# Gate and up projections of both feed-forward layers in seven block products, tokens in two groups of 528

## What is computed

```python
xp = xp + swiglu(rmsnorm(xp, norm_ffn[l]), w_gate[l], w_up[l], w_down[l])
xs = xs + swiglu(rmsnorm(xs, norm_ffn[l]), w_gate[l], w_up[l], w_down[l])
...
def swiglu(h, wg, wu, wd):
    return (jax.nn.silu(h @ wg) * (h @ wu)) @ wd
```

## Time and profile before

| | us |
|---|---|
| median of 3 runs | 3070.7 |
| the profiled execution | 3068.67 |
| its span, first to last instruction | 3066.9 |
| PE busy in the span | 2811.2 |
| DVE / ACT / POOL busy | 1320.3 / 705.3 / 182.7 |
| PE from first to last matmul of the feed-forward of layer 0 | 924.36 to 1703.15 |

### The profile page before, as it was taken

One profiled execution on the slowest core, in us unless ns is written; L12 is line 12 of the kernel. 1 busy time (PEld: TensorE's weight loads), 2 busy tenths in 40 slices (PEclk: granted clock), 3 DMA queues, 4 the chain that ended last, 5 costly groups with the idle time before them and its releaser, 6 DMA issues. The chain is left out here.

```text
span 3066.9 us, 39415 instructions
## 1 busy us (share of the span) xinstructions
PE 2811.2 (92%) x16574; PEld 2587.3 (84%) x16574; DVE 1320.3 (43%) x1977; ACT 705.3 (23%) x1272; POOL 182.7 (6%) x150
## 2 busy tenths in 40 slices
PE   7999999669799999999999699677889999999998
PEld 5866767647699999999999699654889999999997
DVE  3258997365333332323332534374342332323334
ACT  4133232445312111111111322222221111111110
POOL 1011211000001000000000100060010000000000
PEclk9999999879899999999999799765989999999999
DMA  5312223361511112111110111101111112111111
GB/s 160 96 53 65 90 70 102 131 231 40 200 35 48 42 42 61 44 42 42 42 54 23 37 42 42 33 1 31 56 46 44 42 42 63 42 42 42 42 49 64
DMA packets 222587, 189.49 MB, mean 62 GB/s; under 512 B 24737, under 2 KB 172709, under 8 KB 222399
## 3 DMA queue, kind: packets, MB, share of 16 engines
q1 hardware_dynamic: 220727, 181.80, 19.9%
q0 software_dynamic: 1680, 5.07, 0.5%
HBM read 153.21 MB, written 33.50 MB: 61 GB/s over the span
## 5 line engine op out<-in xcount | busy, mean ns | idle before, releaser
L2684 DVE TENSOR_TENSOR xt<-ps,xt 128x1056 f32<-128x1056 f32 x176 | 221.1, 1256 | 204.1 <-PE ps L2468 204.1
L2468 PE MATMUL ps<-ffn_high,f_whG 128*128 128x352 f32 x1056 | 230.1, 326 | 12.3 <-DVE ffn_low L2398 7.8
L2468 PE MATMUL ps<-f_hidh,f_whD 128*128 128x352 f32 x1056 | 228.6, 325 | 9.9 <-DVE f_wlD L2663 9.9
L2468 PE MATMUL ps<-ffn_low,f_whG 128*128 128x352 f32 x1056 | 229.4, 325 | 0.0
L2468 PE MATMUL ps<-ffn_low,f_whU 128*128 128x352 f32 x1056 | 228.7, 324 | 0.0
L2468 PE MATMUL ps<-f_hidh,f_wlD 128*128 128x352 f32 x1056 | 228.4, 324 | 0.0
L2468 PE MATMUL ps<-f_hidl,f_whD 128*128 128x352 f32 x1056 | 228.2, 324 | 0.0
L2468 PE MATMUL ps<-ffn_high,f_whU 128*128 128x352 f32 x1056 | 227.8, 324 | 0.0
L2468 PE MATMUL ps<-ffn_high,f_wlG 128*128 128x352 f32 x1056 | 227.2, 324 | 0.0
L2468 PE MATMUL ps<-ffn_high,f_wlU 128*128 128x352 f32 x1056 | 226.6, 323 | 0.0
L508 PE MATMUL ps<-pe_wh,even_high 128*128 128x512 f32 (+1 forms) x504 | 206.2, 409 | 3.4 <-POOL pe_wl L367 3.1
(11 more groups left out here) (511 smaller groups left out, 4348.6 us busy)
## 6 DMA issues: line engine op xcount, KB each, us to landing
pe_w<-in_w_in_even_dram SPq DMA_DIRECT2D x56, 256.0 KB, 2.8
proj<-pe_out SPq DMA_DIRECT2D x56, 256.0 KB, 2.0
ht_even<-in_w_gate_dram SPq DMA_DIRECT2D x22, 512.0 KB, 5.1
ht_even<-in_w_up_dram SPq DMA_DIRECT2D x22, 512.0 KB, 6.4
ht_even<-in_w_down_dram SPq DMA_DIRECT2D x22, 512.0 KB
ht_odd<-in_w_gate_dram SPq DMA_DIRECT2D x22, 512.0 KB, 5.2
ht_odd<-in_w_up_dram SPq DMA_DIRECT2D x22, 512.0 KB, 6.5
ht_odd<-in_w_down_dram SPq DMA_DIRECT2D x22, 512.0 KB
```

Source lines behind the costliest of these rows:

```text
L2468: last = pe.matmul(g.ps[0:out_rows, b0 + c, 0:THIRD], lhs, rhs[:, c * THIRD:(c + 1) * THIRD], start=(first and n == 0), stop=(final and n ...
L2684: dve.tensor_tensor(xv, g.ps[:, 3 * (m % 2):3 * (m % 2) + 3, 0:THIRD], xv, ALU.add).then_inc(added, 1)
```

## The change

With A the 256 hidden channels by 1024 inputs of a chunk and B the inputs by 528 tokens, both are cut into 2 by 2 blocks, and the four output blocks come from seven block products in place of eight (the variant with 4 sums on either side). So `stage_ffn` is written anew:
- The tokens go in two groups of 528 (`HALF`), each in two quarters of 264 (`QUARTER`). There are 22 steps n for a layer (11 chunks by 2 groups), and all three weight matrices are loaded, cast and split once per group, twice in all. A load of gate or up is now one of 1 MB for the whole chunk.
- PE: 7 products of gate and 7 of up for each n (`product`, 12 matmuls of 264 columns each), into six PSUM banks in turn; the down projection of step n - 1 in 16 units of 6 matmuls (`down`), in the two other banks, two units behind each of eight of the products. That is 264 matmuls for a step, 5808 for a layer.
- POOL makes 4 weight sums for each matrix and step (`add`, 512 elements a partition) and two of the output sums for each (`cross`, 264 elements).
- ACT casts 14 blocks of 512 elements a step (`cast`) and the down tile twice (`cast_down`), copies 4 products out of PSUM (`copy`), and makes two silus and two casts of 528 (`activate`, `hid`).
- DVE: 14 subtractions of 512 (`low`, called by `lower` for step n + 1), 2 of 1024 (`low_down`), 10 output sums from PSUM (`join`, 264), 2 multiplications and 2 subtractions of 528 (`multiply`, `hid`) and 16 additions to the residual (`add`, 264).
- The token blocks of a group are made once: 8 scalings of 528 (`scale`), 4 differences of 1056 (`difference`), 7 casts and 7 subtractions of 1056 (`token`). `open_first` does it for the first group, `open_second` for the second, at n = 11.
- The first gate chunk is loaded at the end of `stage_project_out`.
- Steps 2 to 8 and 12 to 19 are hardware loops of one step each (7 and 8 turns), the others stand unrolled.

The diff, cut, with the indentation of the added lines shortened (of the removed lines, which are functions of `stage_ffn` before, none is shown):

```diff
+    sp.wait_ge(split, KD)
+    sp.dma_start(g.ht[:, 0:2, :].rearrange("p k n -> p (k n)")[:, 0:2048].rearrange(
+        "p (k n) -> p k n", k=KD),
+                 g.ins["w_gate"][layer][:, 0:2 * P].rearrange("(k p) n -> p k n", p=P)
+                 ).then_inc(g.first_gate, 16)
...
+    JOINED_AT = {"G": {2: 1, 3: 2, 4: 3, 5: 4, 6: 5}, "U": {2: 1, 3: 2, 4: 3, 5: 4, 6: 6}}
+    MULTIPLIED = (5, 7)
+    LOW_ORDER = (0, 1, 3, 4, 2, 5, 6)
...
+def group_chunks(fori, chunk):
+    chunk(0, 0)
+    chunk(1, 0)
+    with fori(0, CHUNKS - 4) as i:
+        chunk(i + 2, 0)
+    chunk(CHUNKS - 2, 0)
+    chunk(CHUNKS - 1, 0)
+    chunk(CHUNKS, 1)
+    with fori(0, CHUNKS - 3) as i:
+        chunk(i + (CHUNKS + 1), 1)
+    chunk(N - 2, 1)
+    chunk(N - 1, 1)
...
+    def chunk(n, group):
...
+            load_down(n - 1, (n - 1) // CHUNKS if isinstance(n, int) else group, 1)
+            if not at(n, N - 2, N - 1):
+                load("G", n + 2, group)
+            load_down(n, group, 0)
+        if not at(n, N - 2, N - 1):
+            load("U", n + 2, group)
...
+    def wait_bank(n, index):
+        if index >= 6:
+            before, index = n, index - 6
+        elif at(n, 0):
+            return
+        else:
+            before, index = n - 1, index + (12 if index < 2 else 6)
+        kind, s = "GU"[index // 7], index % 7
+        if s < 2:
+            pe.wait_ge(copied, 4 * before + COPIES[kind] + s + 1)
+        else:
+            pe.wait_ge(joined[kind], JOINS[kind] * before + JOINED_AT[kind][s])
+    def product(kind, s, n, group):
+        index = FIRST[kind] + s
+        pe.wait_ge(weight_low[kind], 7 * n + LOW_COUNT[s])
+        if at(n, 0, CHUNKS) and kind == "G":
+            pe.wait_ge(token_low, 7 * group + s + 1)
+        if at(n, 0) and index == 5:
+            pe.wait_ge(rep_kept, 1)
+        wait_bank(n, index)
+        out = g.ps[:, index % 6, 0:QUARTER]
+        for j in range(4):
+            a, b = slice(j * P, (j + 1) * P), slice(j * QUARTER, (j + 1) * QUARTER)
+            pe.matmul(out, wh[kind][:, s, a], g.hh[:, s, b], start=(j == 0), stop=False)
+            pe.matmul(out, wh[kind][:, s, a], g.hl[:, s, b], start=False, stop=False)
+            last = pe.matmul(out, wl[kind][:, s, a], g.hh[:, s, b], start=False, stop=(j == 3))
+        last.then_inc(done[kind], 1)
+    def down(n, unit):
+        half, m, t = unit // 8, unit // 2 % 4, unit % 2
+        if unit == 0:
+            pe.wait_ge(hid_low, 2 * n + 2)
+        if unit % 8 == 0:
+            pe.wait_ge(down_low, 2 * n + half + 1)
+        if unit >= 2 or not at(n, 0):
+            pe.wait_ge(added, 16 * n + unit - 1)
+        out, b = g.ps[:, 6 + t, 0:QUARTER], slice(t * QUARTER, (t + 1) * QUARTER)
+        for k in range(2):
+            pe.matmul(out, dh[:, k, m, :], hidh[:, k, b], start=(k == 0), stop=False)
+            pe.matmul(out, dh[:, k, m, :], hidl[:, k, b], start=False, stop=False)
+            last = pe.matmul(out, dl[:, k, m, :], hidh[:, k, b], start=False, stop=(k == 1))
+        last.then_inc(down_made, 1)
+    def chunk(n, group):
+        if at(n, CHUNKS):
+            for u in range(8):
+                down(n - 1, u)
+        u = 8 if at(n, CHUNKS) else 0
+        for kind in "GU":
+            for s in range(7):
+                product(kind, s, n, group)
+                if not at(n, 0) and u < 16 and s in ((3, 4, 5, 6) if kind == "G" else (2, 3, 4, 5)):
+                    down(n - 1, u)
+                    down(n - 1, u + 1)
+                    u += 2
+    group_chunks(pe.Fori, chunk)
+    for u in range(16):
+        down(N - 1, u)
...
+    def add(kind, s, n):
+        pool.wait_ge(raw_in[kind], 16 * n + 16)
+        if not at(n, 0):
+            pool.wait_ge(done[kind], 7 * n - 6 + s)
+        if s in (2, 5):
+            pool.wait_ge(sums[kind], 4 * n + {2: 1, 5: 2}[s])
+        out = four(wsum[kind][:, s, :])
...
+    def cross(kind, n, f):
+        pool.wait_ge(copied, 4 * n + COPIES[kind] + 2)
...
+                pool.wait_ge(hid_low, 2 * n - 1 + f)
+        out = (gate if kind == "G" else prod)[:, f, 1, :]
+        pool.tensor_tensor(out, keep[:, 2 + f, :], keep[:, 1, :], ALU.add).then_inc(crossed, 1)
+    def chunk(n, group):
+        if at(n, 0):
+            for kind in "GU":
+                for s in (1, 2, 4, 5):
+                    add(kind, s, 0)
+        for kind in "GU":
+            if not at(n, N - 1):
+                add(kind, 1, n + 1)
+                add(kind, 2, n + 1)
+            cross(kind, n, 0)
+            cross(kind, n, 1)
+            if not at(n, N - 1):
+                add(kind, 4, n + 1)
+                add(kind, 5, n + 1)
...
+    def cast(kind, s, n):
...
+            src = four(wsum[kind][:, s, :])
+        if not at(n, 0):
+            act.wait_ge(done[kind], 7 * n - 6 + s)
+        act.copy(four(wh[kind][:, s, :]), src).then_inc(weight_high[kind], 1)
...
+            token(1, 4)
+            token(1, 5)
+            token(1, 6)
+        else:
+            cast_down(2 * n - 2, 0, at(n, 1))
+            copy("G", 0, n)
+            copy("G", 1, n)
+        prepare("G", 0, 1, 2, 3, 4)
+        activate(n, 0)
+        prepare("G", 5)
+        activate(n, 1)
+        prepare("G", 6)
+        if not at(n, 0, CHUNKS):
+            cast_down(2 * n - 1, 1)
+        copy("U", 0, n)
+        copy("U", 1, n)
+        prepare("U", 0, 1, 2, 3, 4, 5)
+        hid(n, 0)
+        hid(n, 1)
+        prepare("U", 6)
...
+    def low(kind, s, n):
...
+        src = block_of(kind, *PLAIN[s]) if s in PLAIN else four(wsum[kind][:, s, :])
+        dve.tensor_tensor(four(wl[kind][:, s, :]), src, four(wh[kind][:, s, :].bitcast(F32)), ALU.subtract
+                          ).then_inc(weight_low[kind], 1)
...
+    def hid(n, f):
+        dve.wait_ge(hid_high, 2 * n + f + 1)
+        dve.tensor_tensor(hidl[:, f, :], prod[:, f, :, :].rearrange("p t n -> p (t n)"),
+                          hidh[:, f, :].bitcast(F32), ALU.subtract).then_inc(hid_low, 1)
...
+    def open_first():
...
+                              ALU.mult).then_inc(diagonal, 1)
+        for s in LOW_ORDER[:3]:
+            low("G", s, 0)
+        for k in range(4):
+            scale(0, k)
+        difference(0, 1)
+        token(0, 0)
+        for k in range(4, 8):
+            scale(0, k)
+        dve.tensor_copy(rep[:, :], replicated[:, HALF:T]).then_inc(rep_kept, 1)
+        difference(0, 2)
+        token(0, 1)
+        difference(0, 4)
+        difference(0, 6)
+        token(0, 2)
+        low("G", 4, 0)
+        low("G", 2, 0)
+        token(0, 3)
+        low("G", 5, 0)
+        token(0, 4)
+        low("G", 6, 0)
+        token(0, 5)
+        token(0, 6)
+        for s in LOW_ORDER:
+    def open_second(n):
+        low_down(2 * n - 2)
+        for k in range(4):
+            scale(1, k)
+            add(n - 1, 0, k)
+        difference(1, 1)
+        add(n - 1, 0, 4)
+        token(1, 0)
+        add(n - 1, 0, 5)
+        scale(1, 4)
+        add(n - 1, 0, 6)
+        scale(1, 5)
+        add(n - 1, 0, 7)
+        scale(1, 6)
+        scale(1, 7)
+        difference(1, 2)
+        token(1, 1)
+        difference(1, 4)
+        difference(1, 6)
+        token(1, 2)
+        low_down(2 * n - 1)
+        for s in range(3, 7):
+            token(1, s)
...
+    def chunk(n, group):
...
+        else:
+            low_down(2 * n - 2)
+        lower("G", 0)
+        join("G", 2, n)
+        join("G", 3, n)
+        lower("G", 1)
+        adds(0)
+        lower("G", 3)
+        join("G", 4, n)
+        adds(2)
+        lower("G", 4)
+        join("G", 5, n)
+        adds(4)
+        lower("G", 2)
+        lower("G", 5)
+        join("G", 6, n)
+        adds(6)
+        lower("G", 6)
+        if steady:
+            low_down(2 * n - 1)
+        lower("U", 0)
+        join("U", 2, n)
+        adds(8)
+        lower("U", 1)
+        join("U", 3, n)
+        adds(10)
+        lower("U", 3)
+        join("U", 4, n)
+        adds(12)
+        lower("U", 4)
+        join("U", 5, n)
+        multiply(n, 0)
+        adds(14)
+        lower("U", 2)
+        hid(n, 0)
+        join("U", 6, n)
+        multiply(n, 1)
+        lower("U", 5)
+        hid(n, 1)
+        lower("U", 6)
```

More of the change, by code:

```diff
@@ L2564, in _ @@
+            group_chunks(sp.Fori, chunk)
+            load_down(N - 1, 1, 1)
         @block.tensor
         def _(pe):
-            def hidden(kind, f, first=False):
-                pe.wait_ge(split[kind], f + 1)
-                for k in range(KD):
-                    if first:
-                        wait_normed(pe, k)
-                    last = split_passes(g, pe, 0 if kind == "G" else 3, wh[kind][:, k * P:(k + 1) * P],
-                                        wl[kind][:, k * P:(k + 1) * P], g.hh[:, k, :], g.hl[:, k, :],
-                                        k == 0, k == KD - 1)
-                last.then_inc(made[kind], 1)
@@ L2592, in chunk @@
-            def chunk(c, par):
-                for half in range(2):
```

(57 more changed lines are left out.)

389 lines of the change are left out of this document (230 added, 159 removed).

## The result

The changed kernel takes 3173.65 us, the median of 4 runs (3170.13 to 3176.99), against 3069.57 for the kernel before beside it: a ratio of 1.034 (95% interval 1.0327 to 1.0352). Forecast were 3063 us and a range of 3015 to 3125. The profiled execution has a span of 3169.9 us, 103 more than before.

The account below looks back on a forecast made before the run. PE's columns were taken to bound both feed-forward stages. A layer was 705.1 + 18 + 27 + 17 + 9 = 776 us against 780, 8 us less for both, giving 3063 us, with a range of 3015 to 3125.

Parts of the forecast that it names:

- PE's work: Feed-forward matmuls: 5808 of 264 columns at 121.4 ns, 705.1 us a layer for 767.0, 62 us less.
- The loop turns: 13 hardware-loop turns a layer: between 0 and 0.8 us each, nearest to zero.
- The places of the waits: In each steady step PE was to wait on `low_down` and on the `join` of U6.
- the mechanism: DVE operations with two SBUF operands and POOL's lock each other out, costing between 0 and 1.0 us a meeting.
- the term of the steady step: PE's loss in a steady step: 0.95 us, between 0 and 2.1, in 19 steps, 18 us a layer.
- The walk: Steady step followed operation by operation from U5's end: G1 0.3 us late, `low_down` costing half of 1.2 us.
- start, change of group, end: PE's losses at a layer's start, at step 11 and at its end: 27, 17 and 9 us.
- The clock: Slower rival: a step's wait of 1.2 us drops PE to 1.2 GHz for some 3 us; 3112 us, chance 0.18.
- The slower rival by the chain: DVE reaches U4's `low` late in each step: 2.1 us a step and 0.8 a loop turn; 3127 us, chance 0.12.
- The rival in which the meetings miss: DVE and POOL don't collide harmfully: no loss in a step, starts 5 us shorter; 3017 us, chance 0.24.

Follow-up runs that it names:

- without sums: Changed kernel with POOL's eight weight sums a step left out, their slots filled from a plain block: 3004.8 us.
- both: Changed kernel with DVE's `join` of U5, the first `low_down` and both `hid` moved ahead of `low` operations wanted only next step: 3149.1 us.
- The last kernel: "and step 0" with POOL's up sums waiting for the second `low_down`, and the last down half put into the gate's buffers: 3030.3 us, ratio 0.987.
- and step 0: Variant with DVE's additions early and slack work reordered (3074.7 us), plus step 0's `join` of G6 and ACT's first up copies moved ahead: 3070.5 us.
- the moves of the table: Successive reorderings of DVE's queue, then POOL's up sums delayed and the end shortened, from the changed kernel: 3173.7 us to 3030.3 us.

## Why the prediction failed

**Right:** PE's work. The matmuls of 264 columns lie 120.6 ns apart (36 starts from 1103.65 to 1107.87), forecast 121.4; with no wait a step takes 32.01 us, forecast 32.05. So 62 us a layer were there to be had. The loop turns: taken at nothing, and they cost nothing (32.01 in the loop and in unrolled step 20 without sums; in the changed kernel 35.38 and 35.27). Why is open: no run varies the length of the body, so what the prediction concludes from its number of instructions is not tested. The places of the waits, the `join` of U6 and `low_down`, and the mechanism, two engines that shut each other out.

**Wrong, first: the term of the steady step**, 0.95 us with bounds of 0 and 2.1; it measured 3.37 (35.38 less 32.01), above the upper bound. (The walk's own entries, 0.3 and half of 1.2, make 0.90.) Three entries of the walk were mis-sized:
- `join` of U5 was to start 0.8 us behind U5; it starts at 2.07 (1149.80 less 1147.73). Of the 1.27 us, 0.77 is `low` of U4 meeting POOL's sum of slot 5, 0.26 the sum's own price (1.29 us, not the 1.03 of the earlier trace rows), the rest lags of 0.1 between engines. The walk let this sum collide with `multiply`, behind the `join`, and not with the `low` ahead of it: one operation too late.
- G1 was to be 0.3 late; it is 1.19. That is 0.9 of the 2.4 us by which the term was missed.
- `low_down` was to end at 10.2 if POOL won both times; it ends at 11.77, and the wait is 1.87 us where 1.2 was the full price. That is another 0.7. I then took half of the 1.2, "since the rows show POOL winning only in its own sequence", another 0.6. POOL's gate sum is released by G1, which comes at the same place in each step, so here POOL wins in every turn of the loops, with 2.30 us for this `low_down` in each: PE waits for `low_down` seven times in seven steps, 11.8 us in all with 1.7 the longest. A meeting in a periodic schedule isn't a chance that comes half of the time.

The late second matmul behind each of the two waits, 0.2 us a step, was not in the walk at all. In the 19 steps this makes 62 us in place of 18, 44 of the 58.5 us by which a layer was missed. Even with both meetings lost in full the walk would have said 1.5 us a step: the larger part of the miss is that it placed `join` of U5 and all behind it too early.

**Second: start, change of group, end**, 30, 25 and 13 us for 27, 17 and 9. At the start the first product comes at 930.99, where 926 was said. 2.8 us of it lie ahead: the stage opens (the first matmul of its norm) at 914.10, before at 911.28, and since it opens at 907.89 without sums, with the same code up to there, this is a spread between executions and not the change. From the opening to the first product it takes 16.9 us, against 14.7 without sums: POOL's up sums, which I had hidden under DVE's work, shut out DVE's small diagonals (below). At step 11 the first down unit stands right behind U6, and waits 6.88 us for the chain `join`, `multiply`, `hid`, `low`, `low_down`; the walk counted DVE's operations there but not this. The end's two waits came as forecast (4.4 and 2.6 us for 4.3 and 2.5); what was missed is the wait before G1 of step 21, 1.3 us, and a lower clock (0.79 in the window below).

**The rivals.** The clock did not drop in the steps of the changed kernel: in 1000 to 1100 us, with about three waits of 1.87 and of 1.19, it was granted in full. It fell where the waits are longer: at the start (0.85 in 940 to 960, 0.66 in 960 to 980), around the change of group, where PE waits 6.88 and 3.79 us, and at the layer's end (columns as in the earlier trace rows):

```profile
1000.00:1100.00 100.00, 91.91 (x744) 90.60 (x743) 82.07 (x132) 37.09 (x66) 40.19 (x34) 1.00 0.26 85
...
1333.30:1366.70 33.40, 22.69 (x145) 21.23 (x146) 30.47 (x39) 10.89 (x14) 5.64 (x5) 0.87 0.15 48
...
1740.00:1759.00 19.00, 15.98 (x96) 15.51 (x96) 8.15 (x17) 1.05 (x1) 0.00 (x0) 0.79 0.10 28
```

That rival was not far off: in the variant "both", a wait of 2.02 us brought the lower level in seven steps, at 1.5 us each.

The slower rival by the chain (3127 us) was the right mechanism, with too small a loss a step and a loop turn that doesn't exist. It had a chance of 0.12, and the range ended at it, though no row excluded a loss above its 2.1 us a step. The rival in which the meetings miss did not come true in any kernel that makes the sums. The last kernel avoids one meeting and puts the others where nothing urgent stands behind them; 3030 was reached, not 3017.

## What to carry to other kernels

- Where two engines can shut each other out, look for every meeting in one period of the schedule, and count it in full: `low_down` met its sum in every turn of both hardware loops of the changed kernel. Its cost is not its length but what stands behind it in the queue: 0.6 us more on a split cost nothing in the kernel before, and 1.1 us more on `low_down` cost PE 1.36 us a step in the variant "and step 0".
- In an in-order queue, what frees a buffer of the bounding engine goes ahead of what prepares the next step. A wait taken away shows up at the next urgent operation until all slack work stands behind the urgent: the moves of the table brought 3174 us to 3030, and none of them alone gave more than 61. A wait that moves can also grow until the clock falls, as it did at 2.02 us.
- Fewer operations on the bounding engine are worth their time only if the engines behind it don't hold it up: the steps that make up the gain of 62 us a layer were measured only with the sums left out (32.01 us), and the last kernel's take 32.46.

## What the runs showed of the hardware

Not only operations with two SBUF operands are shut out. At the start of layer 0 DVE makes nine small diagonals, each from one SBUF tile and a scalar a partition; in the kernel before they take 0.28 us each, here four of the nine take 1.25 to 1.31, beside POOL's sums (6.08 us for nine, in the timeline):

```profile
917.60 6.08 DVE L2935 TENSOR_SCALAR ht_even<-cst,f_inverse 128x128 f32<-128x128 f32 x9
917.94 1.28 POOL L2694 TENSOR_TENSOR f_wsumG<-ht_even,f_wsumG 128x512 f32<-128x512 f32 x1
...
923.61 0.67 DVE L2841 TENSOR_TENSOR f_wlG<-ht_even,f_whG 128x512 fp32r<-128x512 f32 x1
923.61 3.00 POOL L2694 TENSOR_TENSOR f_wsumU<-ht_even,f_wsumU 128x512 f32<-128x512 f32 x1
924.21 0.67 DVE L2841 TENSOR_TENSOR f_wlG<-f_wsumG,f_whG 128x512 fp32r<-128x512 f32 x1
```

Who wins is not settled. From 923.61 on, POOL's sum takes 3.00 us, and three splits of DVE at their price pass it; in the steady step the sum at 1156.81 gets the port between two of DVE's operations that stood queued, and again in the last kernel at 1104.12. The Trainium skill, SBUF - State Buffer, section "SBUF: two separate sides", says that whoever starts first holds the pair for the whole instruction; the trace agrees on the whole instruction (2.33 us for 0.05 us of being late), but that leaves open who is next when both wait, and no run here settles it.
